# Routing of an expert layer for both token halves in one pass, with softmax weights, row addition and function loads moved

## The reference

```python
# first block, after a state-space mixer and a Fourier mixer
logits = tok @ w_router + b_router                # 256 x 32
top_logit, top_idx = lax.top_k(logits, 4)         # 4 of 32 experts
top_w = softmax(top_logit)
...                                               # tokens sorted by expert
gate, up = split(xe @ w_gate_up[e] + b_gate_up[e])
act = (clip(up) + 1) * min(gate, 7) * sigmoid(1.702 * min(gate, 7))
y = (act @ w_down[e] + b_down[e]) * weight
out = rmsnorm(x + g2 * sum over the 4 experts of y)
# second block: two layers of four mixers; the first has a dense
# feed-forward part, the second 2 of 8 experts of width 1408
probs = softmax(h @ router); top_p, top_i = top_k(probs, 2)
out = layer_norm(ALPHA * h + sum of the 2 experts' outputs)
```

## Time and profile before

| | |
|---|---|
| median of 3 runs | 3097.54 us (3095.83 to 3099.95) |
| the profiled execution | 3097.39 us, span 3095.7 us |
| TensorE busy | 2927.9 us, 95% of the span |
| VectorE, ScalarE, GpSimd busy | 1100.9, 517.0, 548.9 us |
| mean granted TensorE clock | 0.972 |
| moved by DMA | 729.04 MB |

### The profile page before, as it was taken

The page is one execution under the profiler, slowest core; times in us unless marked ns, Lnnn a source line. Parts: engine busy times, 40 slices in busy tenths (PEclk is TensorE's granted clock), DMA queues, the critical chain, the costliest instruction groups (busy, mean ns, idle before and its releaser), DMA issues.

```text
span 3095.7 us, 39180 instructions
## 1 busy us (share of the span) xinstructions
PE 2927.9 (95%) x16071; PEld 1571.6 (51%) x16071; DVE 1100.9 (36%) x1826; ACT 517.0 (17%) x878; POOL 548.9 (18%) x679
## 2 busy tenths in 40 slices
PE   7999999987999999999999979998999999799995
PEld 4447666873333333333333347877887778433331
DVE  4664354123333333333333314461011546321122
ACT  2112132012010111110100112232001332211111
POOL 1000342001322322323223220111110011000001
PEclk9998999997999999999999989999999999799998
DMA  7434311343999999999999962123343211499994
GB/s 253 146 109 167 109 55 55 136 153 123 357 394 396 395 394 397 395 395 397 395 395 397 388 220 89 48 82 112 137 131 127 100 49 41 175 388 386 383 385 166
DMA packets 332915, 729.04 MB, mean 236 GB/s; under 512 B 16004, under 2 KB 61664, under 8 KB 332592
## 3 DMA queue, kind: packets, MB, share of 16 engines
q1 hardware_dynamic: 322160, 699.45, 61.0%
q0 software_dynamic: 10160, 26.77, 2.5%
q10 hardware_dynamic: 400, 0.15, 0.0%
HBM read 709.53 MB, written 16.78 MB: 235 GB/s over the span
## 4 chain that ended last, share of the span: by engine, by line
PE 68%; DMA 3%; DVE 2%; ACT 1%; issue 1%; SPq 1%; POOL 0%; POOLq 0%; DVEq 0%; ACTq 0%; PEldq 0%
PE P L755 66%; DMA WS<-in_w_gate_up 2%; PE P L758 2%; DVE R L1660 1%; SPq L673 1%; ACT R L2389 1%; ACT L2389 0%; DMA R<-expert_rows,small 0%; DVE R L1666 0%; ACT xT L2389 0%; DMA expert_rows<-R 0%; ACT ea L2389 0%; DVE R L1663 0%; DVE xT L1666 0%; POOL R L2943 0%
## 5 line engine op out<-in xcount | busy, mean ns | idle before, releaser
L755 PE MATMUL P<-R 128*64 128x512 f32 (+9 forms) x6484 | 1245.4, 490 | 49.3 <-DVE R L1666 12.9
L755 PE MATMUL P<-WS,R 128*64 128x512 f32 (+4 forms) x4456 | 1006.6, 587 | 6.8 <-POOLq L2854 2.8
L755 PEld LDWEIGHTS P<-R 128*64 128x64 f32 (+4 forms) x6484 | 525.6, 144 | 499.7 <-issue 456.9
L755 PEld LDWEIGHTS P<-WS,R 128*64 128x64 f32 (+2 forms) x4456 | 312.5, 129 | 621.6 <-issue 606.5
L2389 ACT ACTIVATE R<-P 128x512 f32<-128x512 f32 (+5 forms) x444 | 232.0, 524 | 1850.0 <-PE P L755 1529.2
L755 PE MATMUL P<-R,WS 128*128 128x256 f32 (+1 forms) x1888 | 505.9, 427 | 8.4 <-ACT R L2389 4.8
L755 PEld LDWEIGHTS P<-R,WS 128*128 128x128 f32 x1888 | 358.0, 192 | 142.4 <-issue 94.4
L1660 DVE TENSOR_TENSOR R<-P,R 64x512 f32<-64x512 f32 (+3 forms) x260 | 171.9, 661 | 699.4 <-ACT R L2389 388.1
L755 PE MATMUL P<-xT,WS 128*128 128x256 f32 (+2 forms) x1728 | 401.1, 385 | 9.5 <-ACT xT L2389 3.5
L755 PEld LDWEIGHTS P<-xT,WS 128*128 128x128 f32 (+2 forms) x1728 | 317.9, 188 | 71.1 <-issue 21.3
L1660 DVE TENSOR_TENSOR R<-R 64x512 f32<-64x512 f32 (+8 forms) x359 | 256.0, 713 | 64.7 <-ACT R L2389 52.4
(11 more groups left out here) (186 smaller groups left out, 922.7 us busy)
## 6 DMA issues: line engine op xcount, KB each, us to landing
WS<-in_w_gate_up SPq DMA_DIRECT2D x192, 1024.0 KB, 11.5
R<-in_w_down SPq DMA_DIRECT2D x128, 1024.0 KB, 12.9
R<-in_w_gate_up SPq DMA_DIRECT2D x64, 1024.0 KB, 14.4
WS<-in_w_in SPq DMA_DIRECT2D x60, 1024.0 KB, 7.4
WS<-in_w_mod SPq DMA_DIRECT2D x24, 1024.0 KB, 8.1
R<-in_moe_w_down SPq DMA_DIRECT2D x23, 1024.0 KB, 9.2
WS<-in_moe_w_gate SPq DMA_DIRECT2D x20, 1024.0 KB, 11.3
WS<-in_moe_w_down SPq DMA_DIRECT2D x17, 1024.0 KB, 8.2
```

What stands on the lines that cost most here:

```text
L755: return nc.tensor.matmul(out, lhsT, rhs, start=start, stop=stop, skip_group_check=True)
```

## The change

The change has four parts.

- Routing for both halves at once: one instruction handles both halves where two did, the masks are signalled right after they are made (`w_ready`), and the counting takes three products instead of five. The exponential is waited for, and the weights are computed (`weights`), after `Gs`. The turn of the weights (`wT0`) moves behind the sweep.
- `Gs` by quarters of 256 slots: a sort job gives 256 features by 256 slots in four matmuls of 256 columns, so the first four jobs need only the first quarter. Offsets and flag (`spans`) come after the second quarter. GpSimd's first column copy waits for four jobs instead of eight.
- After the first sweep the gathers are issued ahead of the `If` (and again inside it), to a buffer in other memory. VectorE multiplies and adds the rows, the last one in two halves. TensorE turns the two sums onto the bias product with the identity, 16 products of 128x128, in four steps of four.
- ScalarE: `preload_act_table` at eleven places, ahead of waits; the gate `GS` is copied raw tile by tile and gets one Sigmoid over all of it ahead of the first `z`.

```diff
-                b = job(f"rkn{i}", 0)
-                mm(b[:, 0:ne], k1("TU"), msk[:, 0, 0:ne])
-                mm(b[:, 32:32 + ne], k1("ones"), msk[:, 0, 0:ne], True, False)
-                mm(b[:, 32:32 + ne], k1("TU"), msk[:, 1, 0:ne], False, True)
-                mm(b[:, 64:64 + ne], k1("ones"), msk[:, 0, 0:ne], True, False)
-                done(mm(b[:, 64:64 + ne], k1("ones"), msk[:, 1, 0:ne], False, True))
+                pe.wait_ge(S("w_ready"), i + 1)
+                b = job(f"rkn{i}", 0)
+                mm(b[:, 0:2 * ne], k1("TU"), msk, True, False)
+                mm(b[:, ne:2 * ne], k1("ones"), msk[:, 0, :], False, True)
+                done(mm(b[:, 64:64 + 2 * ne], k1("ones"), msk))
+            def place(b, q, p, rows):
+                pe.wait_ge(S("G_half"), q)
+                cols = slice(256 * ((q - 1) % 4), 256 * ((q - 1) % 4) + 256)
+                for kk in range(2):
+                    for c in range(2):
+                        at = 128 * (2 * p + kk)
+                        last = mm(b[:, 256 * kk:256 * kk + 256], rows[:, c, at:at + 128], Gs[:, c, cols], c == 0, c == 1)
+                done(last)
...
+            def turn_back(i, topk, rows):
+                for c in range(2):
+                    for h in range(2):
+                        pe.wait_ge(S("diag_ready"), 2 * c + h + 1)
+                        for m in range(4 * h, 4 * h + 4):
+                            last = mm(acc(m)[:, 128 * c:128 * c + 128], rows[:, c * topk, 128 * m:128 * m + 128], ident, False, True)
+                        if c:
+                            last.then_inc(S("acc_done"), 1)
...
+                for c in range(2):
+                    V(v.max(out=top8[:, c, :], in_=lg[:, c, :]))
+                mark(ts(nmax.unsqueeze(2), top8[:, :, 0:1], -1.0, None, ALU.mult, ALU.bypass), "lg_ready")
+                V(tt(gt, lg, wide(top8[:, :, topk - 1:topk]), ALU.is_gt))
+                V(tt(eq, lg, wide(top8[:, :, topk - 1:topk]), ALU.is_equal))
+                V(v.reduce_sum(need, gt, mybir.AxisListType.X))
+                V(ts(need, need, -1.0, float(topk)))
+                V(v.tensor_tensor_scan(flat(pre), flat(keep), flat(eq), 0.0, ALU.mult, ALU.add))
+                V(tt(pre, pre, wide(need.unsqueeze(2)), ALU.is_le))
+                V(tt(pre, pre, eq))
+                mark(tt(msk, gt, pre, ALU.add), "w_ready")
                 slots(i, ne, topk)
...
-                for hh in range(topk // 2):
-                    cols = slice(512 * hh, 512 * hh + 512)
+                for q in range(topk):
+                    cols = slice(256 * q, 256 * q + 256)
...
+                    if q == 1:
+                        spans(i, ne, topk)
+                weights(i, ne)
...
-            sweeps(dve, a_sweep, 0)
-            diagonals(8)
-            dve.wait_ge(S("acc_done"), 2)
+            sweeps(dve, a_sweep, 0, again=lambda: dve.wait_ge(S("redone0"), 16 * 2 * TOPK))
+            n, b = ready("wT0")
+            F(n, v.tensor_copy(wTt[0:NEXP, :], b[0:NEXP, 0:N]))
+            for c in range(2):
+                dve.wait_ge(S(f"back{back_group(c * TOPK, TOPK)}"), back_value(0, c * TOPK, TOPK))
+                first = back[:, c * TOPK, :]
+                V(ts(first, first, wk[:, c * TOPK:c * TOPK + 1], None, ALU.mult, ALU.bypass))
+                for k in range(1, TOPK - 1):
+                    V(combine(0, TOPK, back, c, k))
+                j = c * TOPK + TOPK - 1
+                dve.wait_ge(S(f"back{back_group(j, TOPK)}"), back_value(0, j, TOPK))
+                for h in range(2):
+                    cols = slice(512 * h, 512 * h + 512)
+                    mark(stt(first[:, cols], back[:, j, cols], wk[:, j:j + 1], first[:, cols], ALU.mult, ALU.add), "diag_ready")
             for m in range(8):
+                if m % 4 == 0:
+                    dve.wait_ge(S("acc_done"), 2 + m // 4)
...
+            def table(f):
+                act_.preload_act_table(f)
...
+                        if i == 0:
+                            A(fn(GS, GS, ACT.Sigmoid))
...
-                        ins = fn(GS[:, i, :], b[:, 0:N], ACT.Sigmoid)
+                        ins = fn(GS[:, i, :], b[:, 0:N], ACT.Copy)
...
-                    pool.wait_ge(S("mm_free"), START["xs"] + 8)
+                    pool.wait_ge(S("mm_free"), START["xs"] + 4)
...
-            sweeps(pool, a_sweep, 0)
-            bring_back(0, TOPK, back)
-            pool.wait_ge(S("acc_done"), 2)
+            sweeps(pool, a_sweep, 0, lambda: bring_back(0, TOPK, back), lambda: landed(pool, 0, TOPK),
+                   lambda: bring_back(0, TOPK, back, True))
+            pool.wait_ge(S("acc_done"), 3)
```

More of the change, by code:

```diff
@@ L261, in build, with pair, routing @@
         WX = reg(2048, 6, 2048)
-        rt = reg(B0, 8, 32)
+        rt = small[:, 640:896].rearrange("p (a b) -> p a b", a=4)
         wr = reg(B0 + 256, KT, 32)
         rb = reg(B0 + 1792, 32)
-        wtok = small[:, 448:512].rearrange("p (c e) -> p c e", c=2)
-        lgs = small[:, 512:576].rearrange("p (c e) -> p c e", c=2)
-        msk = small[:, 576:640].rearrange("p (c e) -> p c e", c=2)
+        top8 = small[:, 320:336].rearrange("p (c e) -> p c e", c=2)
+        nmax, need, den = (small[:, 336 + 2 * i:338 + 2 * i] for i in range(3))
+        most = small[:, 342:343]
+        def pair(at, ne):
+            return small[:, at:at + 2 * ne].rearrange("p (c e) -> p c e", c=2)
+        def routing(ne):
+            return [pair(at, ne) for at in (448, 512, 576, 384)]
         act = reg(B0 + 7060, FFE, N)
@@ L1328, in _ @@
             sweeps(pe, a_sweep, 0)
+            pe.wait_ge(S("slots_ready"), 1)
+            b = job("wT0", 0)
+            for c in range(2):
+                last = turn(b[0:NEXP, 128 * c:128 * c + 128], routing(NEXP)[0][:, c, :])
+            done(last)
+            empty_all()
             open_sum(lambda m: bdn[0:NEXP, 128 * m:128 * m + 128], lambda m: wTt[0:NEXP, :])
-            gather_back(0, TOPK, back)
+            turn_back(0, TOPK, back)
             squared("ss3", sqb, 1)
@@ L1602, in _ @@
                     router(1, 8, xk)
-                    pe.wait_ge(S("G_half"), 3)
                     for i in range(8):
-                        b = job("xm", i)
-                        for c in range(2):
-                            last = mm(b[:, :], xrow[:, c, 128 * i:128 * i + 128], Gs[:, c, 0:512], c == 0, c == 1)
-                        done(last)
+                        place(job("xm", i), i // 4 + 5, i % 4, xrow)
                 empty_all()
@@ L1889, in slots @@
             def slots(i, ne, topk):
+                wtok, lg, msk, keep = routing(ne)
+                key = pair(32, ne)
                 n, b = ready(f"rkn{i}")
```

144 lines of the change are left out of this document (63 added, 81 removed).

## The result

The changed kernel takes 3067.47 us (median of four runs, 3065.57 to 3070.15) beside 3096.68 us for the kernel before (3094.46 to 3099.95): a ratio of 0.9905, 95% interval 0.9888 to 0.9923. The forecast was 3067.0. The profiled execution took 3070.15 us, its span 3068.4; of the kernel before, 3095.7.

The account below looks back on a forecast made before the run. TensorE, busy 95% of the span, bounds the kernel, so gains come from its waits or removed work. 10.9 + 8.3 + 8.8 + 1.0 + 1.3 + 0.7 - 0.5 = 30.5 off 3097.4 gives 3067; range 3059 to 3075.

Parts of the forecast that it names:

- First routing: Ahead of the first sweep: earlier counting, quarters and a hidden GpSimd copy gain 10.9 us, between 8.5 and 12.
- Way back: Behind the first sweep: earlier gathers and VectorE's sums gain 8.3 us up to the projection, bounds 5 and 10.
- where the gathers stand ahead of the `If`, the same place shows 0.81: Second block's interval taken for the first gather after the first sweep: 6.53 falls to 0.81, gathers move by 6.4 us.
- Second routing: Second block: counting right behind ScalarE's last copy, so the product behind the sort starts 8.8 us earlier.
- The clock's part: First product behind the second routing's sort: less low clock after shorter idle, 1.0 us more gain, between 0 and 1.4.
- Function loads: Loads ahead of waits: 1.3 us gained before the last logarithm, 0.7 behind the two layers' head norms.
- The one Sigmoid: State-space part, ahead of the first `z`: one Sigmoid of 2048 columns loses 0.5 us, range 0 to 2.4.
- The clock's rival: TensorE stays at 1.2 GHz through squares and into projection, second sweep starts cold: about 3072.5 us; chance 0.13.
- The preload: Rival: preload brings logarithm and exponential together, saving six second loads, 7.7 us, so 3059.5; chance 0.07.
- The weight stream: Rival: in the sweeps loads come late and TensorE waits at all 32 visits; at 1.1 us each, 3102; chance 0.03.
- One sign: After the first sweep: a first gather within 1 us of the last rows' landing would show the prediction right.
- one sign of being wrong: Way back: TensorE waiting for VectorE's additions beyond 1841 us, counted without the earlier gain, would show the prediction wrong.

Follow-up runs that it names:

- the cure: Changed kernel plus one more gather on GpSimd at the ninth expert of the first block's sweep, into an unread region: 3068.06 us, ratio 0.9903.
- five waits: Changed kernel plus five waits on GpSimd, which wait for nothing, at the ninth expert of the first sweep: 3069.09 us, ratio 0.9903.
- a plain load: Changed kernel plus a load of 128 rows without row indices on GpSimd, at the ninth expert, into an unused region: 3064.99 us, ratio 0.9901.

## Why the prediction was right

The total was forecast as 3067.0 and is 3067.47; the gain summed to 30.5, measured as 29.2 by the medians and 27.3 by the two profiled executions (1.8 us of the shortfall is the start). The waits that were to shrink did shrink, in every part, but the terms were not all right. That the total agrees to half a microsecond is luck: the way back alone was 2.6 too high, and one kernel's executions differ by 4 us.

- **First routing**, forecast 10.9, measured 11.33. Counting right behind ScalarE's last copy, the quarters at 3.9, the copy hidden: each as forecast. The runs split it: 1.9 to the quarters, 2.0 to the copy, the rest, some 7, to masks of both halves at once and counting ahead of the weights.
- **Way back**, forecast 8.3, measured 5.71. The failed step is "where the gathers stand ahead of the `If`, the same place shows 0.81": the second block's interval was taken for the price without the `If`. It is 3.98 here, 3.2 of it a pause of GpSimd's DMA queue. By the count of transfers it belongs in the same place in the kernel before, inside its 6.53. The `If` is worth 3.5, and the gathers started 3.3 earlier instead of 6.4. From the landing of the last expert's rows to the projection the forecast had 30.65 (38.95 before, less 8.3); it took 32.53: 3.1 more in the interval, 0.2 more to the seventh gather's landing, 0.4 less from there to the squares, 0.5 less in the squares (3.92 instead of 4.4), 0.1 less behind them, and 0.4 less for a colder start of the projection, which did not come (granted clock 0.63 in its first 2.35 us, 0.58 before). What VectorE's hold on two gathers cost lies somewhere in that 0.2; no run shows it alone. So 6.4 were gained from the landing on, and 0.7 lost ahead of it, to a low clock in the last expert's products: 5.71.
- **Second routing**, forecast 8.8 up to the first product and 1.0 for the clock in it; the first was measured as 9.76. Counting took 0.81 instead of 1.40, and the sort 16.35. The clock's part came as forecast in its place (the first product took 11.23 instead of 12.88, 1.65 less) but not in the end: from its start to the last rows' gather the two kernels differ by 0.14, and where the 1.65 went is open.
- **Function loads**, forecast 2.0, measured 2.1 by the run without them; but 0.2 of it lie in layer norms, and the second layer's head norms gave nothing. The one Sigmoid over the four tiles, 1.9 us on ScalarE, cost nothing instead of 0.5: from the first 75 us to the first router product both kernels take 622.94 us.
- **Rivals.** The clock's rival came in part: the first identity step ran at the low clock, the squares nearly at the high one, and the second sweep began at it. The Trainium skill, "TensorE: Matmul & The Clock Gate", section "Why this matters for your kernels", has the rule that I cited for it; by that alone one would have taken the low end, 5 us, and 5.71 is near it, but for another reason: the squares ran at 0.95. The preload did not bring both functions: each logarithm's load is still followed by an exponential's, though by naming the set it could. The weight stream did not take over at the new start (-0.20 us over the sweep), but it is closer than I held: half a megabyte more shows as 1.2 us.
- **Signs.** One sign did not come: the first gather was not within 1 us of its rows. And one sign of being wrong did: TensorE waited for VectorE's additions until 1832.14, which is 1841.9 without the earlier gain (9.75 at the last expert's turn), beyond the 1841 that was to say that the prediction is wrong: 3.1 us of that are the longer interval.

The range of 3059 to 3075 held it.

## What to carry to other kernels

Where an engine's interval vanishes once in a trace and stands elsewhere, don't take the small one for its price without the cause removed: here the same place held a branch (3.5 us) and a pause of the queue (3.2 us), and only runs with each changed alone parted them. And look at what a gap is at the same instruction elsewhere: of 3.82 us that seemed a pause, 3.1 were a wait that comes every time. A control that lengthens the code as the cure does (five waits), and one that loads the queue as much (a plain load), are cheap, and each of them struck out a theory. Where a logarithm and an exponential follow each other, name the set that has both: on the path it was worth more per line changed than anything else here.

## What the runs showed that I had not expected

- GpSimd pauses ahead of the 129th and the 159th transfer that it issues, by their number and not by its code or their bytes: 0.74 us and 3.2 us on top of the usual gap in the changed kernel, 0.80 and 0.97 in all with one more transfer ahead of them.
- A gather's issue takes 0.94 us, and up to 1.71 when it starts while VectorE works on 1024 columns.
- In the sweep, at 395 GB/s, the weight stream has no slack: 0.52 MB from another queue cost TensorE 1.2 us.
- Identical code differs by up to 3.6 us between executions in the second block's layers (788.2 to 791.8 us), and the same stretch of 60 us has a granted clock of 0.94 in one and 1.00 in the other. An edit of 2 us can't be read from medians of five runs; in the trace it can.
